# Latent attention: keys made for two heads and values for four heads at once, with the first values behind the first two score rows

## The chip, the cores and the metric

The kernel runs on one core of a Trainium2 chip. The metric is the device time of one execution in microseconds (us). The kernel is one program with its five engines (TensorE, VectorE, ScalarE, GpSimd, SyncE) programmed by hand: each engine has its own instruction list, which it works off in order, and they wait for one another through semaphores.

## The reference, cut to what matters

The model is two blocks; only the latent attention in the first layer of the first one is touched. For 1024 tokens and 8 heads:

```python
q = einsum('bsr,re->bse', rmsnorm(c_q, q_norm), w_uq)        # 256 -> 8 x (64 + 32)
kv = einsum('bsr,re->bse', rmsnorm(c_kv, kv_norm), w_ukv)    # 128 -> 8 x (64 + 64)
k_nope, v = kv[..., :64], kv[..., 64:]
s = (q_nope @ k_nope.T + rope(q_rope) @ rope(k_rope).T) * scale   # k_rope is one for all heads
p = softmax(where(causal, s, -inf))
y = p @ v
```

Everything before it (input projection, recurrent part) and after it (output product, layer norm, a state space layer, a second attention, a feed-forward part) stays as it is.

## The kernel before, in words

**Precision.** Every float32 operand of a product is split into a high part (rounded) and a low part (the rest), and three products are summed: high by high, low by high, high by low. ScalarE makes high parts by a copy, VectorE or GpSimd makes low parts by a subtraction. So a product of a head needs, after TensorE, a copy and a subtraction out of PSUM before it can be used.

**Weights.** They come in slabs of 128 x 1024 numbers, one DMA each from SyncE. GpSimd splits each (`split`, one cast and four subtractions) as soon as the slab two before it is released (semaphore `s_slab`). Each head has one slab: queries in tiles 0 and 1, and in tile 2 the 64 key columns and the 64 value columns of this head.

**The attention stage** is a loop over the heads u = 0 to 7, written out for each engine. "Body u" below is one pass of it. Body u computes the attention of head u and, between its parts, makes queries, keys and values of head u + 1 (`head_queries`, `head_keys`, `head_values`). Body 7 has no next head and makes none of these. Scores come in eight rows of 128 queries each (i = 0 to 7, `MLA_ROWS` gives their order, the long ones first). For a row: `score_rows` on TensorE, `neg_max` on VectorE, `exponentials` on ScalarE, `invert` on VectorE, `divide` on ScalarE. Then ten chunks (c = 0 to 9) of the probabilities are turned by TensorE (`turn_chunk`), split by ScalarE (`chunk_hi`) and VectorE (`chunk_lo`), and multiplied with the values (`chunk_values`). Chunks 0 to 3 need rows 0 and 1, chunks 4 to 6 rows 2 and 3, chunks 7 and 8 rows 4 and 5, chunk 9 rows 6 and 7.

**The order on TensorE** (in body u): score row 0, chunk 7 of the head before, row 1, chunk 8 of the head before, turn 9 of the head before, queries of u + 1, chunk 9 of the head before, row 2, turns 0 and 1, row 3, chunk 0, turn 2, keys of u + 1, chunk 1, turn 3, row 4, chunk 2, turn 4, row 5, chunk 3, turn 5, values of u + 1, chunk 4, turn 6, row 6, chunk 5, turn 7, row 7, chunk 6, turn 8. Body 0 has no parts of a head before. Queries, keys and values of head 0 stand ahead of the loop.

**The PSUM ring.** Score rows and the products for queries, keys and values share two pairs of banks, taken in turn (`MLA_RING`). A use waits until the use two before it is finished with (`ring_freed`): for a score row, until its exponential is done; for queries, until `q_turned` is done; for keys and values, until their low part is made (`s_kvl`).

**ScalarE in a body**: exponential 0, divide 0, chunk_hi 9 of before, exponential 1, divide 1, then chunk_hi 0, exponential 2, chunk_hi 1, exponential 3, chunk_hi 2, divide 2, `k_hi`, divide 3, chunk_hi 3, exponential 4, chunk_hi 4, exponential 5, chunk_hi 5, `q_hi`, `v_hi`, divides 4 and 5, chunk_hi 6 and so on. VectorE goes the same way, with `k_lo` behind `neg_max` 4 and `v_lo` behind `invert` 5. GpSimd makes the low part of the queries (`q_lo`).

**Keys.** A key tile (`KH`, `KL`) has the 64 own columns of the head in partitions 0 to 63 and the rotated common part in partitions 64 to 127. The common part is written once into each of two buffers ahead of the loop; head u uses buffer u % 2. `VM` holds the values of two heads, high and low part side by side.

## Time and profile before

| what | value |
|---|---|
| median of 3 runs | 2646.82 us (2643.38 to 2647.17) |
| span of the profiled execution | 2643.2 us |
| TensorE busy | 2572.9 us, 12880 matmuls |
| VectorE busy | 1599.2 us |
| ScalarE busy | 1001.6 us |
| GpSimd busy | 1140.9 us |
| attention stage, from the first queries to the last chunk | about 202 to 413 us of the span |

The profile gives no time of its own for the profiled execution beside its span; the three timed runs lie 0.2 to 4.0 us above the span. In the rows, "busy" of TensorE is the time in which at least one matmul was in flight, and matmuls overlap: a row's duration of one matmul is longer than the distance between two. A TensorE row of a timeline that says x2 or x8 is a run of that many matmuls, and its start against the start of the next row is the time they take.

### The profile page before, as it was taken

Reading aid. Unit: us, or ns where it says so; the run is one execution under the profiler, and the core shown is the slowest. Engines: PE = TensorE matmul, PEld = TensorE weight load, DVE = VectorE, ACT = ScalarE, POOL = GpSimd, SP = SyncE. Lnnn points to the kernel's source line nnn. Section 1 sums busy time; section 2 is a strip of 40 time slices with the busy share of each in tenths; the row PEclk is TensorE's granted clock in tenths of the full one; section 3 lists DMA queues with packets and bytes.
Section 4 is the critical chain, followed back from the end, with each engine's and each line's share of the span. In section 5 each row is a group of like instructions: output and inputs, shape, how many; then the busy total and the mean of one; then the engine's idle time right before and its main releaser. Section 6 shows DMA issues by size and latency. Waiting matters only on the chain.

```text
span 2643.2 us, 33209 instructions
## 1 busy us (share of the span) xinstructions
PE 2572.9 (97%) x12880; PEld 2055.9 (78%) x12880; DVE 1599.2 (61%) x1936; ACT 1001.6 (38%) x1434; POOL 1140.9 (43%) x1422
## 2 busy tenths in 40 slices
PE   8999999999999999999999999999999999999998
PEld 6877878687787787877776777767888888888886
DVE  6636663777647648557776455564455565555556
ACT  3527881436405315225365445563201111111132
POOL 4633344532432432432442222214565557655653
PEclk9999999999999999999999999999999999999999
DMA  3110002212112112111230010003111111111312
GB/s 139 48 51 27 24 25 90 86 59 100 52 55 73 58 49 71 66 59 66 90 112 24 25 33 25 33 17 104 56 49 48 48 56 56 54 43 49 120 47 80
DMA packets 44822, 156.36 MB, mean 59 GB/s; under 512 B 4928, under 2 KB 5312, under 8 KB 44672
## 3 DMA queue, kind: packets, MB, share of 16 engines
q1 hardware_dynamic: 31392, 110.11, 12.8%
q10 hardware_dynamic: 13280, 44.17, 4.6%
q8 instruction: 103, 1.69, 0.3%
q14 instruction: 47, 0.39, 0.0%
HBM read 141.55 MB, written 12.71 MB: 58 GB/s over the span
## 4 chain that ended last, share of the span: by engine, by line
PE 85%; DVE 8%; ACT 4%; issue 2%; POOL 1%; ACTq 0%; DVEq 0%; POOLq 0%
PE PS L784 38%; PE PS L1459 13%; PE PS L1485 10%; PE PS L1114 4%; PE PS L1021 3%; PE PS L1507 2%; PE PS L1347 1%; PE PS L920 1%; PE PS L1330 1%; PE PS L1147 1%; PE PS L1157 1%; PE PS L1151 1%; PE PS L934 1%; PE PS L1370 1%; DVE mla_neg_max L2397 1%
## 5 line engine op out<-in xcount | busy, mean ns | idle before, releaser
L637 POOL CAST w_hi<-w_stage 128x1024 fp32r<-128x1024 f32 x130 | 145.0, 1115 | 1048.4 <-PE PS L784 758.2
L640 POOL TENSOR_TENSOR w_lo<-w_stage,w_hi 128x256 fp32r<-128x256 f32 x520 | 492.9, 979 | 10.4
L784 PE MATMUL PS<-XH,w_hi 128*128 128x512 f32 x1216 | 386.7, 399 | 9.0 <-ACT ssd_z L1899 3.3
L784 PE MATMUL PS<-XL,w_hi 128*128 128x512 f32 x1216 | 375.9, 390 | 0.0
L784 PE MATMUL PS<-XH,w_lo 128*128 128x512 f32 x1216 | 375.4, 390 | 0.0
L784 PEld LDWEIGHTS PS<-XH,w_hi 128*128 128x128 f32 x1216 | 221.5, 188 | 65.4 <-issue 12.9
L784 PEld LDWEIGHTS PS<-XH,w_lo 128*128 128x128 f32 x1216 | 228.3, 188 | 48.7
L784 PEld LDWEIGHTS PS<-XL,w_hi 128*128 128x128 f32 x1216 | 228.3, 188 | 48.6
L711 POOL TENSOR_TENSOR w_lo<-w_stage,w_hi 128x256 fp32r<-128x256 f32 x260 | 220.1, 853 | 0.0
L707 POOL CAST w_hi<-w_stage 128x256 fp32r<-128x256 f32 x260 | 125.7, 486 | 185.6 <-PE PS L1459 108.2
L1459 PE MATMUL PS<-raw_hi,w_hi 128*128 128x512 f32 x512 | 158.2, 390 | 0.0
L1459 PE MATMUL PS<-raw_hi,w_lo 128*128 128x512 f32 x512 | 157.8, 389 | 0.0
L1459 PE MATMUL PS<-raw_lo,w_hi 128*128 128x512 f32 x512 | 157.7, 389 | 0.0
L1485 PE MATMUL PS<-ffn_u_hi,w_hi 128*128 128x512 f32 x392 | 152.6, 389 | 0.0
L1485 PE MATMUL PS<-ffn_u_hi,w_lo 128*128 128x512 f32 x392 | 152.6, 389 | 0.0
L1485 PE MATMUL PS<-ffn_u_lo,w_hi 128*128 128x512 f32 x392 | 152.6, 389 | 0.0
L3032 DVE TENSOR_TENSOR H<-H,PS 128x512 f32<-128x512 f32 x140 | 96.1, 686 | 76.9 <-PE PS L1485 76.9
L2973 DVE SCALAR_TENSOR_TENSOR ffn_t<-PS,root 128x1024 f32<-128x1024 f32 x32 | 39.2, 1225 | 154.2 <-PE PS L1459 145.0
L2176 ACT ACTIVATE ffn_t<-ffn_t 128x1024 f32<-128x1024 f32 x32 | 34.0, 1061 | 240.1 <-DVE ffn_t L2973 240.1
L1459 PEld LDWEIGHTS PS<-raw_hi,w_hi 128*128 128x128 f32 x512 | 96.1, 188 | 20.3 <-issue 0.5
L1459 PEld LDWEIGHTS PS<-raw_lo,w_hi 128*128 128x128 f32 x512 | 96.1, 188 | 19.9
L1459 PEld LDWEIGHTS PS<-raw_hi,w_lo 128*128 128x128 f32 x512 | 96.1, 188 | 19.9
(459 smaller groups left out, 5421.5 us busy)
## 6 DMA issues: line engine op xcount, KB each, us to landing
w_stage<-w SPq DMA_DIRECT2D x202, 512.0 KB, 3.4
ssd_sum_rows<-sums_kept ACTq DMA_DIRECT2D x32, 512.0 KB, 3.7
H<-x_t ACTq DMA_DIRECT2D x8, 512.0 KB, 8.3
pj_kept<-ple_proj_tiles ACTq DMA_DIRECT2D x8, 512.0 KB, 2.6
h_kept<-H ACTq DMA_DIRECT2D x8, 512.0 KB, 3.0
H<-h_kept ACTq DMA_DIRECT2D x4, 1024.0 KB, 5.5
out_t<-out_tiles SPq DMA_DIRECT2D x16, 256.0 KB, 2.1
x_again<-x_t ACTq DMA_DIRECT2D x12, 256.0 KB, 3.1
```

Source lines behind the costliest of these rows:

```text
L637: nc.gpsimd.tensor_copy(w_hi[:, slot, :, :], w_stage[:, slot, :, :]).then_inc(s_w_hi, 1)
L640: nc.gpsimd.tensor_tensor(w_lo[:, slot, k:k + 2, :], w_stage[:, slot, k:k + 2, :], w_hi[:, slot, k:k + 2, :].bitcast(F32), ALU.subtract).t ...
L707: nc.gpsimd.tensor_copy(ring(w_hi, e), src).then_inc(s_eh.sem, 1)
L711: nc.gpsimd.tensor_tensor(ring(w_lo, e), src, ring(w_hi, e).bitcast(F32), ALU.subtract).then_inc(done, count)
L784: mm = nc.tensor.matmul(outs[:, half, :], wt[:, slot, k, :], a[:, k - first, half * HB:(half + 1) * HB], start=(k == whole[0] and wt is w_ ...
L1021: mm = nc.tensor.matmul(PS[:, 2 * (n % 2) + half, :], wt[:, n % 2, k, :], a[:, k, half_cols(half)], start=(k == 0 and wt is w_hi and a is ...
L1114: mm = nc.tensor.matmul(PS[:, half, :], wt[:, n % 2, k, :], a[:, k, half * HB:(half + 1) * HB], start=(k == 0 and wt is w_hi and a is XH), ...
L1459: mm = nc.tensor.matmul(PS[:, 2 * (c % 2) + half, :], ring(wt, e + k // 2, k % 2), a[:, k, half * HB:(half + 1) * HB], start=(k == 0 and w ...
L1485: mm = nc.tensor.matmul(PS[:, BANK[j], :], ring(wt, e + i, k), a[:, ACTS_AT[j], k, :], start=(j not in BEFORE and k == 0 and wt is w_hi an ...
L1507: mm = nc.tensor.matmul(PS[:, 4 + 2 * e + half, :], ring(wt, e0 + k // 2, k % 2), a[:, t, half * HB:(half + 1) * HB], start=(first and wt ...
L2973: v.scalar_tensor_tensor(out=FT[:, c % 2, :], in0=flat(c % 2), scalar=0.0, in1=RSQ[:, :], op0=ALU.max, op1=ALU.mult).then_inc(s_ue, 1)
L3032: v.tensor_tensor(dst, dst, src, ALU.add).then_inc(s_dr, 1)
```

## The change

The weights of a head's slab are laid out anew on the host: tile 2 holds the keys of two heads (slabs of heads 0, 2, 4, 6), tiles 3 and 4 hold the values of four heads (slabs of heads 0 and 4). The number of slabs and their size stay.

- `head_keys` runs for even heads only and fills all 128 rows of the output: head u in partitions 0 to 63, head u + 1 in 64 to 127. Its six matmuls keep their 512 columns. `k_hi` and `k_lo` then make two copies and two subtractions, one for each head. There are three key buffers (head u uses u % 3), so a third copy and a third subtraction of the common rotated part come ahead of the loop.
- `head_values` runs for heads 0 and 4. It has two parts (j = 0, 1) of 512 tokens each, with 12 matmuls of 256 columns per part in place of 24 of 64 columns per head. Each part takes a turn in the ring and is split by itself. The values of head 4 go to a tile of their own (`VM4`), since head 3 is not finished with when they are made; those of 5 to 7 take the places of 0 to 2.
- The values of head 0 to 3 are made in body 0 behind score row 1 and ahead of the queries of head 1, no longer ahead of the loop; `v_hi(0)` stands behind `divide(0, 1)` on ScalarE, `v_lo(0)` behind `invert(0, 1)` and ahead of `q_turned(1)` on VectorE.
- The last product that reads a head's slab releases it: keys or values for even heads, the queries for odd heads.
- The rotated key part waits at another address (`KF`) until it is copied.

```diff
-MLA_RING = [("q", 0), ("k", 0), ("v", 0)]
+KEY_HEADS, VALUE_HEADS = 2, 4
+MLA_RING = [("q", 0), ("k", 0)]
+MLA_PARTS = [("rope", 0, 0), ("rope", 1, 0), ("rope", 2, 0), ("k", 0, 0), ("k", 0, 1)]
 for _u in range(MLA_H):
     for _i in range(8):
         MLA_RING.append((_i, _u))
-        if _i in (1, 3, 5) and _u + 1 < MLA_H:
-            MLA_RING.append(({1: "q", 3: "k", 5: "v"}[_i], _u + 1))
+        if _i == 1 and _u == 0:
+            MLA_RING += [("v", 0, 0), ("v", 0, 1)]
+            MLA_PARTS += [("v", 0, 0), ("v", 0, 1)]
+        if _u + 1 == MLA_H:
+            continue
+        if _i == 1:
+            MLA_RING.append(("q", _u + 1))
+        if _i == 3 and (_u + 1) % KEY_HEADS == 0:
+            MLA_RING.append(("k", _u + 1))
+            MLA_PARTS += [("k", _u + 1, _e) for _e in range(KEY_HEADS)]
+        if _i == 5 and (_u + 1) % VALUE_HEADS == 0:
+            MLA_RING += [("v", _u + 1, 0), ("v", _u + 1, 1)]
+            MLA_PARTS += [("v", _u + 1, 0), ("v", _u + 1, 1)]
...
+        def value_places(u):
+
+            if u == 0:
+                return [(VM, 0, 0, VALUE_HEADS)]
+            return [(VM4, 0, 0, 1), (VM, 0, 1, VALUE_HEADS)]
...
             def head_values(u):
-                n, b = N_HEADS + u, 2 * mla_pair(("v", u))
-                ring_freed(("v", u))
-                for a, wt in ((CKH, w_hi), (CKH, w_lo), (CKL, w_hi)):
-                    for t in range(KT):
-                        mm = nc.tensor.matmul(PS[:, b, 64 * t:64 * t + 64], a[:, t * P:(t + 1) * P], wt[:, n % 2, 2, 64:128],
-                                              start=(t == 0 and a is CKH and wt is w_hi), stop=True, skip_group_check=True)
-                mm.then_inc(s_slab, 1)
+                if u % VALUE_HEADS:
+                    return
+                n = N_HEADS + u
+                for j in range(2):
+                    b = 2 * mla_pair(("v", u, j))
+                    ring_freed(("v", u, j))
+                    for a, wt in ((CKH, w_hi), (CKH, w_lo), (CKL, w_hi)):
+                        for t in range(4):
+                            tok = slice((4 * j + t) * P, (4 * j + t + 1) * P)
+                            mm = nc.tensor.matmul(PS[:, b + t // 2, t % 2 * 256:t % 2 * 256 + 256], a[:, tok],
+                                                  wt[:, n % 2, 3:5, :].rearrange("p a b -> p (a b)"),
+                                                  start=(t % 2 == 0 and a is CKH and wt is w_hi), stop=True, skip_group_check=True)
+                    mm.then_inc(s_hp if j == 0 else s_slab, 1)
...
             head_queries(0)
             head_keys(0)
-            head_values(0)
             for u in range(MLA_H):
                 more = u + 1 < MLA_H
                 score_rows(u, 0)
                 if u:
                     chunk_values(u - 1, 7)
                 score_rows(u, 1)
+                if u == 0:
+                    head_values(0)
...
             def k_hi(u):
-                act.wait_ge(s_hp, 2 * u + 2)
-                nc.scalar.activation(KH[0:64, u % 2, :], flat(mla_pair(("k", u)))[0:64, :], ACT.Copy).then_inc(s_kvh, 1)
+                if u % KEY_HEADS:
+                    return
+                head_product(act, "k", u)
+                for e in range(KEY_HEADS):
+                    nc.scalar.activation(KH[0:64, (u + e) % 3, :], flat(mla_pair(("k", u)))[64 * e:64 * e + 64, :], ACT.Copy).then_inc(s_kvh, 1)
...
             def v_hi(u):
-                act.wait_ge(s_slab, N_HEADS + u + 1)
-                nc.scalar.activation(VM[:, u % 2, :, 0:64], PS[:, 2 * mla_pair(("v", u)), :].rearrange("p (t d) -> p t d", d=64),
-                                     ACT.Copy).then_inc(s_kvh, 1)
+                if u % VALUE_HEADS:
+                    return
+                for j in range(2):
+                    if j == 0:
+                        head_product(act, "v", u, 0)
+                    else:
+                        act.wait_ge(s_slab, N_HEADS + u + 1)
+                    if u == 0 and j == 0:
+                        act.wait_ge(s_kvl, 3)
+                    for t, at_, h0, h1 in value_places(u):
+                        done = nc.scalar.activation(value_part(t, at_, h1 - h0, j, 0), value_bank(u, j, h0, h1), ACT.Copy)
+                    done.then_inc(s_kvh, 1)
...
-            v_hi(0)
             nc.scalar.preload_act_table_set("natural_log_exp_and_others")
...
                 if u:
                     low_part(u - 1, 0)
                 else:
+                    v_hi(0)
                     gated_hi(2)
...
                 invert(u, 1)
+                if u == 0:
+                    v_lo(0)
                 if more:
                     q_turned(u + 1)
```

## Rows read from the trace of the kernel before

**Rows 1.** The page: busy time of each engine, share of the span, instructions.

```profile
PE 2572.9 (97%) x12880; PEld 2055.9 (78%) x12880; DVE 1599.2 (61%) x1936; ACT 1001.6 (38%) x1434; POOL 1140.9 (43%) x1422
```

**Rows 2.** Windows: stretch, length, busy time (instructions) by engine, granted clock, DMA.

```profile
210.00:235.00 25.00, 24.26 (x148) 19.89 (x148) 14.60 (x26) 21.39 (x36) 7.76 (x8) 0.93 0.09 30
260.00:285.00 25.00, 24.16 (x167) 20.50 (x166) 17.20 (x33) 20.14 (x39) 11.11 (x9) 1.00 0.07 22
```

**Rows 3.** Timeline, TensorE, body 2: chunk 9, row 3, turns 4, 5, 7.

```profile
267.81 0.34 PE L949 MATMUL PS<-mla_p_hi,mla_v_hi_lo 128*128 128x256 f32 x2
...
270.12 0.60 PE L920 MATMUL PS<-mla_k_hi,mla_q_hi 128*128 128x512 f32 x2
...
276.50 0.66 PE L934 MATMUL PS<-CN,mla_p 128*128 128x128 f32 x4 [0.60 <-ACT mla_p L1684]
...
278.47 0.62 PE L934 MATMUL PS<-CN,mla_p 128*128 128x128 f32 x4
...
283.49 0.66 PE L934 MATMUL PS<-CN,mla_p 128*128 128x128 f32 x4
```

**Rows 4.** Timeline, TensorE, body 7: the same five places.

```profile
391.20 0.45 PE L949 MATMUL PS<-mla_p_hi,mla_v_hi_lo 128*128 128x256 f32 x2 [2.35 <-DVE mla_p_lo L2408]
...
395.21 0.60 PE L920 MATMUL PS<-mla_k_hi,mla_q_hi 128*128 128x512 f32 x2
...
400.91 0.66 PE L934 MATMUL PS<-CN,mla_p 128*128 128x128 f32 x4 [0.30 <-ACT mla_p L1684]
...
402.64 0.61 PE L934 MATMUL PS<-CN,mla_p 128*128 128x128 f32 x4
...
405.98 0.66 PE L934 MATMUL PS<-CN,mla_p 128*128 128x128 f32 x4
```

**Rows 5.** Timeline, TensorE, body 2: keys, chunk 1, turn 3; values, chunk 4.

```profile
272.34 0.70 PE L898 MATMUL PS<-ckv_hi,w_hi 128*64 128x512 f32 x2
...
273.80 0.40 PE L949 MATMUL PS<-mla_p_hi,mla_v_hi_lo 128*128 128x256 f32 x2
...
274.28 0.49 PE L934 MATMUL PS<-CN,mla_p 128*128 128x128 f32 x3
...
278.85 1.06 PE L907 MATMUL PS<-w_hi,ckv_hi 128*128 128x64 f32 x8
...
281.53 0.48 PE L949 MATMUL PS<-mla_p_hi,mla_v_hi_lo 128*128 128x256 f32 x2
```

**Rows 6.** Timelines of ScalarE and VectorE, body 2, and ScalarE, body 7.

```profile
274.61 1.01 ACT L1668 ACTIVATE mla_k_hi<-PS 64x1024 fp32r<-64x1024 f32 x1
275.52 0.93 ACT L1684 ACTIVATE mla_p<-mla_p,mla_sums 128x768 f32<-128x768 f32 x1
...
280.09 1.06 ACT L1664 ACTIVATE mla_q_hi<-mla_q 128x1024 fp32r<-128x1024 f32 x1
281.73 0.60 ACT L1672 ACTIVATE mla_v_hi_lo<-PS 128x512 fp32r<-128x512 f32 x1 [0.58 <-PE PS L907]
282.22 1.22 ACT L1684 ACTIVATE mla_p<-mla_p,mla_sums 128x384 f32<-128x384 f32 x2
...
275.88 1.21 DVE L2388 TENSOR_TENSOR mla_k_lo<-PS,mla_k_hi 64x1024 fp32r<-64x1024 f32 x1
...
404.26 0.62 ACT L1684 ACTIVATE mla_p<-mla_p,mla_sums 128x384 f32<-128x384 f32 x1
```

**Rows 7.** Ahead of the loop: rope subtractions, `q_turned(0)`, score row 0 of head 0.

```profile
L2379 DVE TENSOR_TENSOR mla_k_lo<-key_rope,mla_k_hi x2: 1223/1641/2059, 201.8 to 202.9; 64x1024 fp32r<-64x1024 f32 x2
...
205.22 1.23 DVE L2383 SCALAR_TENSOR_TENSOR mla_q<-PS,trig 128x1024 f32<-128x1024 f32 x1 [0.27 <-PE PS L784]
...
210.02 0.68 PE L920 MATMUL PS<-mla_k_hi,mla_q_hi 128*128 128x512 f32 x2 [0.65 <-POOL mla_q_lo L654]
```

**Rows 8.** Body 0: score row 2, the divide of row 1, `q_turned(1)`.

```profile
217.48 0.56 PE L920 MATMUL PS<-mla_k_hi,mla_q_hi 128*128 128x512 f32 x2
...
217.66 1.15 ACT L1684 ACTIVATE mla_p<-mla_p,mla_sums 128x1024 f32<-128x1024 f32 x1 [0.23 <-DVE mla_sums L2403]
...
217.62 1.23 DVE L2383 SCALAR_TENSOR_TENSOR mla_q<-PS,trig 128x1024 f32<-128x1024 f32 x1
```

More of the change, by code:

```diff
@@ L170 @@
         MLA_RING.append((_i, _u))
-        if _i in (1, 3, 5) and _u + 1 < MLA_H:
-            MLA_RING.append(({1: "q", 3: "k", 5: "v"}[_i], _u + 1))
+        if _i == 1 and _u == 0:
[11 more added lines that the diff above has]
+            MLA_PARTS += [("v", _u + 1, 0), ("v", _u + 1, 1)]
+HEAD_PRODUCTS = [_k for _u in range(MLA_H) for _k in
+                 (("q", _u), ("k", _u), ("v", _u, 0)) if _u % {"q": KEY_HEADS, "k": VALUE_HEADS, "v": VALUE_HEADS}[_k[0]] == 0]
 MLA_TURN = {_key: _n for _n, _key in enumerate(MLA_RING)}
@@ L177, in mla_high, with mla_part, key_part @@
     return MLA_HIGHS.index(key) + 1
+def mla_part(kind, u, e=0):
+    return MLA_PARTS.index((kind, u, e)) + 1
+def key_part(u):
+    return mla_part("k", u - u % KEY_HEADS, u % KEY_HEADS)
 def mla_pair(key):
@@ L751, in _, with head_product, value_weights, value_part @@
                 plain_slab(n)
+        def head_product(eng, *key):
+            if key in HEAD_PRODUCTS:
+                eng.wait_ge(s_hp, HEAD_PRODUCTS.index(key) + 1)
+            else:
+                eng.wait_ge(s_slab, N_HEADS + key[1] + 1)
+        def value_places(u):
+            if u == 0:
+                return [(VM, 0, 0, VALUE_HEADS)]
+            return [(VM4, 0, 0, 1), (VM, 0, 1, VALUE_HEADS)]
+        def value_weights(u, kt):
+            if u < VALUE_HEADS:
+                return VM[:, u, kt, :]
+            return VM4[:, 0, kt, :] if u == VALUE_HEADS else VM[:, u - VALUE_HEADS - 1, kt, :]
+        def value_part(t, first, heads, j, o):
+            return t[:, first:first + heads, 4 * j:4 * j + 4, o:o + 64].rearrange("p h t d -> p t h d")
+        def value_bank(u, j, h0, h1):
+            return flat(mla_pair(("v", u, j))).rearrange("p (t h d) -> p t h d", t=4, d=64)[:, :, h0:h1, :]
         class Tiles:
@@ L874, in ring_freed @@
                     return
-                kind, u = MLA_RING[turn - 2]
+                kind, u = MLA_RING[turn - 2][:2]
                 if kind == "q":
@@ L888, in head_queries @@
                 ring_freed(("q", u))
-                product(pair(mla_pair(("q", u))), n, CQH, CQL, range(2), ready=None if u else (s_llo, 0)).then_inc(s_hp, 1)
+                mm = product(pair(mla_pair(("q", u))), n, CQH, CQL, range(2), ready=None if u else (s_llo, 0))
+                mm.then_inc(s_hp if ("q", u) in HEAD_PRODUCTS else s_slab, 1)
             def head_keys(u):
+                if u % KEY_HEADS:
+                    return
                 n, b = N_HEADS + u, 2 * mla_pair(("k", u))
@@ L948, in chunk_values @@
                         late = P if e and p == i else 0
-                        mm = nc.tensor.matmul(PS[:, b, q0 + late:q0 + 2 * P], VM[:, u % 2, 2 * p + e, :],
+                        mm = nc.tensor.matmul(PS[:, b, q0 + late:q0 + 2 * P], value_weights(u, 2 * p + e),
                                               src[:, n % 4, 2 * P * e:2 * P * (e + 1) - late],
@@ L1652, in _ @@
             act.wait_ge(s_kr, 3)
-            for b in range(2):
+            for b in range(3):
                 nc.scalar.activation(KH[64:128, b, :], KF[64:128, :], ACT.Copy).then_inc(s_kvh, 1)
@@ L2376, in _ @@
                 v.tensor_tensor(lo, CQ[:, j, :], hi.bitcast(F32), ALU.subtract).then_inc(s_llo, 1)
-            for b in range(2):
+            for b in range(3):
                 dve.wait_ge(s_kvh, b + 1)
@@ L2386, in k_lo @@
             def k_lo(u):
[L2387 to L2393 removed]
+                if u % KEY_HEADS:
+                    return
+                for e in range(KEY_HEADS):
+                    at_ = (u + e) % 3
+                    dve.wait_ge(s_kvh, mla_part("k", u, e))
+                    v.tensor_tensor(KL[0:64, at_, :], flat(mla_pair(("k", u)))[64 * e:64 * e + 64, :], KH_f[0:64, at_, :], ALU.subtract).then_inc(s_kvl, 1)
+            def v_lo(u):
+                if u % VALUE_HEADS:
+                    return
+                for j in range(2):
+                    dve.wait_ge(s_kvh, mla_part("v", u, j))
+                    for t, at_, h0, h1 in value_places(u):
+                        done = v.tensor_tensor(value_part(t, at_, h1 - h0, j, 64), value_bank(u, j, h0, h1),
+                                               value_part(t, at_, h1 - h0, j, 0).bitcast(F32), ALU.subtract)
+                    done.then_inc(s_kvl, 1)
             def neg_max(u, i):
@@ L2416, in _ @@
             k_lo(0)
-            v_lo(0)
             v.memset(SM[:, 5, 0:1], 0.0).then_inc(s_evac[1], MLA_H // 2)
```

40 lines of the change are left out of this document (21 added, 19 removed).

## The prediction

> **What bounds the kernel now.** The page comes first. TensorE is busy for 97% of the span [rows 1], so the obvious reading is that TensorE time taken out is time won. The change touches one stage only, the latent attention (about 202 to 412 us of 2643), so I then read that stage by windows [rows 2]. In a steady stretch ScalarE is busy 20 of 25 us and VectorE 17 of 25. Neither is full, but both work in a fixed order, and TensorE's order alternates between matmuls that need nothing and matmuls that wait for them. The third view is TensorE's timeline of one steady pass, the body of head 2 [rows 3]. Its one wait in these rows looks small: 0.60 us before `turn_chunk(2, 4)`, for a divide on ScalarE.
>
> The row that decides is elsewhere. The body of head 7 makes no queries, keys or values for a next head, since there is none, so it is a body with this filling work taken out. I compare the same places in both bodies, from the score row of i = 3 on [rows 3, 4]:
> - score row 3 to chunk turn 4: 276.50 - 270.12 = 6.38 us with a key product between, 400.91 - 395.21 = 5.70 us without. Saved: 0.68 us, though the key product takes 1.46 us of TensorE.
> - chunk turn 4 to chunk turn 5: 1.97 against 1.73 us. Saved: 0.24 us. Score row 5 waits for a key split in one and not in the other.
> - chunk turn 5 to chunk turn 7: 5.02 us with the value product (2.68 us), 3.34 us without.
> So the filling products sit largely in time that the softmax chain (scores, maximum, exponential, divide, turn, high part, low part) takes anyway. TensorE looks 97% busy because the filling fits, not because it is the bound.
>
> **The change, TensorE's work.** A head's 24 value matmuls take 281.53 - 278.85 = 2.68 us, 112 ns each for 64 columns; four 256-column matmuls with the same kind of weights take 274.28 - 273.80 = 0.48 us, 120 ns each [rows 5]. Eight value products (21.4 us) become 48 matmuls of 256 columns (5.8 us). Four key products of eight go, at 273.80 - 272.34 = 1.46 us each: 5.8 us. In all 21.4 us less TensorE work. On this the Trainium skill would differ: TensorE: Matmul & The Clock Gate, "Back-to-back issue gap", prices a matmul by its columns, N / 2.4 + 2.5 ns, which is 29 ns for 64 columns and 109 ns for 256; by that (an estimate) the values would cost 5.6 us before and 5.2 after and save nothing. The measured 112 ns of these very instructions contradicts it, and nothing below uses it.
>
> **What of it reaches the end, body by body** ("body u" computes head u and makes the products of head u + 1).
>
> Bodies 2, 4 and 6 lose keys and values but keep the queries. They become like body 7 plus one `q_hi` on ScalarE. There `divide(7, 4)` starts at 404.26 [rows 6]; `q_hi` (1.0 us) would stand in its place, and the two divides (1.22 us together [rows 6]) would end at 406.45, so turn 7 is 406.45 - 402.64 = 3.81 us after turn 5 and not 5.02. Gain per body 0.68 + 0.24 + 1.21 = 2.13 us; three bodies 6.4 us.
>
> Bodies 1 and 5 keep a key product, now with two halves to split, and lose the values. ScalarE issues a second `k_hi` (0.91 us from one start to the next [rows 6]) ahead of `divide(u, 3)`, for which turn 4 already waits: +0.9 us. VectorE's second `k_lo` (1.21 us [rows 6]) stands in front of `chunk_lo(3)`, and score row 5 waits for both splits: another 0.15. Everything to exponential 5 and `q_hi` is then 1.05 us late. Behind `q_hi`, the wait for the values (0.58 us idle) and `v_hi` (0.49 us until the divide) are gone: 1.07 back. Net 0.0 to 0.2, I take 0.1 each.
>
> Body 3 has both: two key splits (+1.05 to `q_hi`), and two value parts of 1024 columns. The values of head 4 go to another tile than those of 5 to 7, so each part is two copies and two subtractions. ScalarE then has about 1.15 us per part before the divides, where it had 0.58 + 0.49 in all. `q_hi` ended at 281.15 in body 2, so ends at 282.2 here; 2.3 for the parts and 1.2 for the divides make 285.7, so turn 7 comes at 285.75 and not 283.49. VectorE needs 1.3 us per part, and score rows 6 and 7 now wait for these subtractions in the ring of PSUM pairs (284.75 and 286.05). Loss 2.4 us.
>
> Body 0 is the place that matters. Today the first values run while the chain query product, `q_turned`, `q_hi`, `q_lo` is under way (TensorE waits 0.65 us at the end [rows 7]), so they cost nothing there. After the change:
> - A third rope part costs ScalarE one copy near 187 us, where it waits anyway, but VectorE one subtraction more before `q_turned(0)`. Such a one takes 1.22 to 2.06 us [rows 7]; VectorE has 0.27 us of idle there. I take the short one, since the long one ran beside GpSimd's work: 0.95 us later. `q_hi`, `q_lo` and score row 0 move by it, from 210.02 to 210.95. TensorE idles from 206.5 on.
> - Part of the 25 us from 210 was at half clock (1.2 GHz): 0.93 granted on average [rows 2], and the first score rows are slow in it. Row 0 then lies in it wholly (0.15 us longer), so the softmax of the first two rows is 1.1 us late: `divide(0, 1)` ends at 218.8 [rows 8] + 1.1 = 219.9.
> - Now the new chain. `v_hi(0)` stands behind `divide(0, 1)` on ScalarE: 1.0 us for 1024 columns, 220.9. `v_lo` 1.23 us (as `q_turned`, also 1024 columns out of PSUM [rows 8]), 222.1. The ring of two PSUM pairs makes `head_queries(1)` wait for the split of the first value half, which held its pair. The queries are twelve matmuls of the kind of which six make a key product (1.46 us): 2.9, so 225.0. Score row 2 waits for the second half (223.3, earlier) and so starts at 225.0, where it started at 217.48 [rows 8]. Before, queries 1 waited only for the exponential of row 0. That is 7.5 us; 0.2 of it comes back because chunk turn 0, right behind row 2, had to wait for that divide's end at 218.81 and now need not. 7.3 us late at score row 3.
> - From there it is a body without keys and values: 2.13 back. Net loss 5.2 us.
> Behind score row 2 in TensorE's queue stand chunk turn 0 and everything of head 0, so nothing fills this.
>
> GpSimd gets its slabs' release earlier for odd heads and 10 us later for head 0. The next slab (about 4 us to split) is wanted a body later: nothing. No DMA is added or removed, and the weights loaded are as many.
>
> **Sum.** +5.2 (body 0) + 2.4 (body 3) - 0.2 (1, 5) - 6.4 (2, 4, 6) = +1.0 us. Against the profiled span of 2643.2 this is 2644.2; the median of the runs shown is 2646.82, 3.6 us over that span, so 2647.8. Behind the attention TensorE has products back to back, so a shift is handed to the end unchanged.
> Bounds: the long rope subtraction +0.85. The value copy at twice its 512-column row (0.60 us [rows 6], so 1.20 for 1024) +0.2. Body 3 with no cover +1. On the good side: the second key split and body 3's value split wholly under other waits, -1.0 each for bodies 1 and 5 and -2.4 for body 3. That is 2643.4 to 2649.9 without the clock.
>
> **Rivals.**
> (a) TensorE is the bound after all. For it: 97% busy, and waits that look small. Then bodies 1, 5 give 2.68 each, bodies 2, 4, 6 give 4.14 each, body 3 nothing, and body 0 loses 7.3 - 4.14 = 3.2: 17.8 - 3.2 = 14.6 us faster, 2632. Against it: from score row 3 to turn 7, body 7 takes 10.77 us and body 2 takes 13.37, only 2.60 less for 4.14 us of matmuls missing, and one copy fewer on ScalarE in it. Chance 0.12.
> (b) Slower: the clock. Body 7 had TensorE idle for 2.35 us, and then a stretch at half clock in which score row 2 and turns 0, 1 took 395.21 - 391.20 = 4.01 us, where body 2 took 270.12 - 267.81 = 2.31: 1.7 us per such stretch [rows 3, 4]. After the change body 0 has two new idle times (before the second value half, and 2 us before queries 1), and bodies 2, 4, 6 have 2 us more idle each. One stretch, in queries 1, is as likely as not and costs 1.2 to 1.7 us: 2649. It takes three to be over the 5.3 us that count as slower; four give 2647.8 + 6.8 = 2654.6. Against that: in bodies 2, 4, 6 the idle comes in pieces of 0.5 to 1 us. Chance of three or more 0.12. The Trainium skill (the same page, "Why this matters for your kernels") also warns of idle gaps between bursts of matmuls as the cause of drops in mid-kernel; this trace shows it at 391 us.
> (c) The first values hurt less than I say, because ScalarE reaches them earlier or the ring wait is shorter, and bodies 1, 3, 5 come out at their good bounds (-4.4): 4 to 9 us better, 2639 to 2644. Chance 0.14.
> My forecast, 2644 to 2652 with at most two new stretches at half clock: 0.62.
>
> **Numbers.** 2647.8 is the likeliest case. The range 2640 to 2654 holds the forecast, most of (c) and part of (b), and leaves (a) out. Over 0.2% (5.3 us, about what measurement tells from no change) faster, below 2641.5, are (a) and a third of (c): 0.17. Slower, above 2652.1, is (b) and the forecast's edge: 0.16. Within: 0.67.
>
> **What the new profile must show.** Queries 1 start near 222 us with a wait for the first value subtraction; score row 2 near 225. From score row 3 to chunk turn 7, bodies 2, 4 and 6 take about 11.2 us (now 13.4), 1 and 5 about as now, body 3 about 15.6. Value matmuls 48, near 120 ns apart. If bodies 2, 4, 6 take about 9.2 there, (a) is right; if half-clock stretches appear in them, (b). I am wrong in the main if ScalarE and VectorE wait for TensorE in body 2 between turn 5 and turn 7.

## The result, and the profile after

Over 19 runs of each, the changed kernel takes 2651.33 us (median; 2646.75 to 2653.68) and the kernel before 2646.80 (2643.06 to 2649.16). The ratio is 1.0020, 95% interval 1.0014 to 1.0026: slower by 3.7 to 6.9 us; the two medians themselves lie 4.5 us (0.17%) apart. The forecast was 2647.8 in a range of 2640 to 2654, with "within 0.2%" as the likeliest. The time lies in the range, 3.5 us above the forecast, and the ratio at the edge of 0.2%, on the slower side. For the change itself the forecast was +1.0 us. Below, one of the eleven runs of x1_rope (9895 us) and one of x3_fill (2879 us) were slow and are in no ratio.

The page of the changed kernel, its first lines (they answer to [rows 1]):

```profile
span 2651.4 us, 32872 instructions
...
PE 2564.2 (97%) x12712; PEld 2044.7 (77%) x12712; DVE 1602.6 (60%) x1935; ACT 1003.8 (38%) x1433; POOL 1142.0 (43%) x1422
```

There are 168 matmuls fewer, all of them in the attention, and the span is longer. TensorE is still "97% busy". Nothing on this page says what happened, so the stage has to be read.

Windows of the changed kernel (stretch, length, busy time and count of TensorE, its weight loads, VectorE, ScalarE, GpSimd, granted clock, DMA). The first two answer to [rows 2]; the last three each hold a stretch at half clock (0.50), in bodies 0, 1 and 3, with some time at full clock around it:

```profile
210.00:235.00 25.00, 20.09 (x95) 16.22 (x95) 13.12 (x18) 16.21 (x23) 5.54 (x6) 0.80 0.14 43
...
260.00:285.00 25.00, 23.01 (x139) 19.27 (x139) 17.27 (x32) 20.57 (x42) 9.08 (x8) 0.93 0.07 22
...
224.00:229.00 5.00, 5.00 (x19) 3.97 (x18) 1.67 (x2) 0.00 (x0) 1.53 (x3) 0.66 0.32 105
...
262.00:266.00 4.00, 4.00 (x23) 3.65 (x21) 2.12 (x5) 2.69 (x6) 0.22 (x1) 0.57 0.02 6
...
309.00:315.00 6.00, 5.80 (x33) 5.42 (x33) 2.89 (x7) 3.99 (x9) 1.33 (x1) 0.72 0.00 0
```

In the first window TensorE is busy for 20.1 us and not 24.3, with 95 matmuls and not 148: this is the hole at the start of the stage. ScalarE and VectorE do less in it too. The granted clock is 0.80 and not 0.93.

TensorE's timeline of the changed kernel: body 0 first (keys 0, score row 0, the two halves of the first values, queries 1, score row 2), then body 2 (score row 3, chunk turns 4, 5, 7, as in [rows 3]), then body 3 (chunk turn 4, the values of heads 4 to 7, the chunk behind them, turn 7):

```profile
206.21 0.61 PE L949 MATMUL PS<-ckv_hi,w_lo 128*128 128x512 f32 x2
211.74 1.11 PE L977 MATMUL PS<-mla_k_hi,mla_q_hi 128*128 128x512 f32 x2 [4.92 <-POOL mla_q_lo L678]
...
217.04 1.17 PE L963 MATMUL PS<-w_hi,ckv_hi 128*128 128x256 f32 x4
...
219.84 0.74 PE L963 MATMUL PS<-w_hi,ckv_hi 128*128 128x256 f32 x4 [0.68 <-ACT mla_p L1748]
...
223.48 0.70 PE L832 MATMUL PS<-cq_hi,w_hi 128*128 128x512 f32 x2 [1.94 <-POOL w_lo L664]
...
224.99 1.06 PE L832 MATMUL PS<-cq_hi,w_hi 128*128 128x512 f32 x2
...
227.55 0.74 PE L977 MATMUL PS<-mla_k_hi,mla_q_hi 128*128 128x512 f32 x2
...
278.27 0.61 PE L977 MATMUL PS<-mla_k_hi,mla_q_hi 128*128 128x512 f32 x2
...
283.98 0.66 PE L991 MATMUL PS<-CN,mla_p 128*128 128x128 f32 x4 [0.30 <-ACT mla_p L1754]
...
285.71 0.61 PE L991 MATMUL PS<-CN,mla_p 128*128 128x128 f32 x4
...
289.55 0.66 PE L991 MATMUL PS<-CN,mla_p 128*128 128x128 f32 x4 [0.59 <-ACT mla_p L1754]
...
308.41 0.66 PE L991 MATMUL PS<-CN,mla_p 128*128 128x128 f32 x4 [1.65 <-ACT mla_p L1754]
...
311.66 1.20 PE L963 MATMUL PS<-w_hi,ckv_hi 128*128 128x256 f32 x4
...
315.00 0.64 PE L963 MATMUL PS<-w_hi,ckv_lo 128*128 128x256 f32 x4
315.48 0.40 PE L1006 MATMUL PS<-mla_p_hi,mla_v_hi_lo 128*128 128x256 f32 x2
...
317.93 0.66 PE L991 MATMUL PS<-CN,mla_p 128*128 128x128 f32 x4
```

Body 0 holds two waits that were not there: 4.92 us before score row 0 (0.65 before, [rows 7]) and 1.94 us before queries 1. In body 2 everything is where it was forecast: row 3 to turn 7 takes 289.55 - 278.27 = 11.28 us.

The other engines' timelines of the changed kernel:

```profile
202.04 4.89 DVE L2449 TENSOR_TENSOR mla_k_lo<-key_rope,mla_k_hi 64x1024 fp32r<-64x1024 f32 x3
206.95 1.23 DVE L2453 SCALAR_TENSOR_TENSOR mla_q<-PS,trig 128x1024 f32<-128x1024 f32 x1
...
222.11 2.35 DVE L2470 TENSOR_TENSOR mla_v_hi_lo<-PS,mla_v_hi_lo 128x1024 fp32r<-128x1024 f32 x2 [2.13 <-ACT mla_v_hi_lo L1742]
...
221.07 1.92 ACT L1742 ACTIVATE mla_v_hi_lo<-PS 128x1024 fp32r<-128x1024 f32 x2
...
204.24 4.63 POOL L664 TENSOR_TENSOR w_lo<-w_stage,w_hi 128x256 fp32r<-128x256 f32 x4
209.34 2.35 POOL L678 TENSOR_TENSOR mla_q_lo<-mla_q,mla_q_hi 128x1024 fp32r<-128x1024 f32 x1 [0.47 <-ACT mla_q_hi L1722]
```

The wait of queries 1 is put down to `w_lo` by the profile, but GpSimd began the next `w_lo` only at 222.72, for the slab of head 2, and those that queries 1 need ended at 208.9. The first of the two `v_lo` (start 222.11, half of 2.35 us) ends at 223.3, and queries 1 start at 223.48: that is the ring of PSUM pairs, as forecast.

Where the difference lies is seen best from the length of each body. A body is taken here from the start of score row 0 of one head to that of the next; the last column is the start of score row 7 of head 7, all in us, each kernel from its own profiled execution.

| kernel | row 0, head 0 | row 2, head 0 | body 0 | 1 | 2 | 3 | 4 | 5 | 6 | row 7, head 7 |
|---|---|---|---|---|---|---|---|---|---|---|
| before | 210.02 | 217.48 | 24.91 | 25.49 | 24.82 | 24.84 | 24.80 | 24.80 | 24.83 | 406.39 |
| after | 211.74 | 227.55 | 31.03 | 25.85 | 22.68 | 28.38 | 22.72 | 25.11 | 22.71 | 412.41 |
| x1_rope | 211.21 | 225.70 | 29.38 | 25.77 | 22.72 | 28.37 | 22.71 | 25.07 | 22.73 | 410.16 |
| x2_ahead | 211.47 | 218.34 | 22.37 | 25.57 | 22.71 | 26.95 | 22.78 | 25.90 | 22.72 | 402.36 |
| x3_fill | 211.31 | 224.66 | 28.23 | 25.57 | 22.68 | 26.98 | 22.79 | 25.70 | 22.70 | 407.84 |
| x4_keys_only | 212.68 | 220.67 | 24.44 | 26.73 | 23.90 | 27.54 | 23.88 | 26.08 | 23.90 | 411.31 |
| x5_values_only | 211.23 | 225.48 | 30.05 | 24.32 | 23.61 | 25.73 | 23.70 | 23.66 | 23.61 | 407.70 |
| x6_before_third | 210.10 | 218.13 | 24.80 | 24.78 | 24.11 | 24.13 | 24.09 | 24.12 | 24.12 | 402.13 |
| x7_late | 209.90 | 216.74 | 22.54 | 25.83 | 22.73 | 28.36 | 22.68 | 25.16 | 22.74 | 402.14 |
| x8_late_qhi | 210.06 | 216.91 | 22.04 | 25.46 | 22.23 | 26.83 | 22.23 | 25.23 | 22.21 | 398.39 |
| x9_before_qhi | 209.82 | 217.54 | 25.20 | 25.49 | 24.77 | 24.80 | 24.77 | 24.80 | 25.99 | 407.95 |
| x10_values_best | 210.27 | 217.12 | 22.62 | 23.83 | 23.13 | 25.58 | 23.12 | 23.14 | 23.13 | 397.03 |

From before to after: row 0 of head 0 +1.72, body 0 +6.12, body 3 +3.54, bodies 1 and 5 +0.67 together, bodies 2, 4, 6 -6.34 together, body 7 +0.3. That is +6.0 us at row 7 of head 7. The two spans differ by 8.2; another 1.6 us came between 546 and 583 us, where the changed kernel's execution had a stretch at half clock (549 to 553 us) among dense products; the kernel before had one at 528 to 532 us, where it cost nothing that shows. The rest came in crumbs. The medians differ by 4.5 us only, so what lies outside the stage belongs to these two executions, and the stage is what is to be explained. Stretches at half clock also come and go between executions of one kernel: the changed kernel's 19 go from 2646.75 us at a granted clock of 0.997 to 2653.68 at 0.992, and the profiled one (2653.21, 0.992) is the second slowest of them.

### The profile page after: what moved, and what is told of

Its sections match the earlier page's. It is cut to its first block, busy times and chain, and to the rows that moved or that the text cites. A ratio compares the mean times of both kernels' runs of the same rounds, so it can differ in the third digit from the quotient of the medians.

```text
span 2651.4 us, 32872 instructions
## 1 busy us (share of the span) xinstructions
PE 2564.2 (97%) x12712; PEld 2044.7 (77%) x12712; DVE 1602.6 (60%) x1935; ACT 1003.8 (38%) x1433; POOL 1142.0 (43%) x1422
## 3 DMA queue, kind: packets, MB, share of 16 engines
q8 instruction: 101, 1.65, 0.3%
## 4 chain that ended last, share of the span: by engine, by line
PE 84%; DVE 9%; ACT 5%; issue 2%; POOL 1%; ACTq 0%; DVEq 0%; POOLq 0%
PE PS L832 38%; PE PS L1517 13%; PE PS L1543 10%; PE PS L1172 4%; PE PS L1079 2%; PE PS L1565 2%; PE PS L1405 1%; PE PS L977 1%; PE PS L1388 1%; PE PS L1205 1%; PE PS L1215 1%; PE PS L1209 1%; PE PS L1428 1%; PE PS L991 1%; DVE mla_neg_max L2476 1%
```

## The experiments

All medians are of runs on one chip beside runs of the kernel before; that kernel's median in the same comparison stands behind "against". It differs from one comparison to the next (2645.46 to 2646.80), so two kernels of different comparisons are set side by side by their distances from it: the changed kernel lies 4.5 us above it. Each ratio is to the kernel before, with its 95% interval.

### Body 0: the rope part, the order, the clock

**x1_rope** moves the third rope subtraction behind `q_turned(0)` on VectorE.

```diff
+            rope_low(0)
+            rope_low(1)
...
             q_turned(0)
+            rope_low(2)
             k_lo(0)
```

> The changed kernel with the third rope subtraction moved on VectorE from ahead of q_turned(0) to behind it, where VectorE waited 2.0 us for the first k_hi. Theory (the subtraction delays the whole head 0 chain): q_turned(0) starts near 205.5 and not 206.95 us, score row 0 near 210.2 and not 211.74, and score row 2 of head 0 1.5 us earlier than 227.55; total 1 to 2 us below the changed kernel, so about 3 us over the kernel before. Rival (score row 0 is not what orders body 0, the clock is): row 0 earlier, row 2 and the total unchanged.

Measured: 2651.42 us against 2645.48, ratio 1.0021 (1.0012 to 1.0031). `q_turned(0)` came back to 205.46, as expected, yet score row 0 started at 211.21, only 0.5 us earlier than in the changed kernel. GpSimd's timeline of this kernel says why:

```profile
204.20 4.65 POOL L664 TENSOR_TENSOR w_lo<-w_stage,w_hi 128x256 fp32r<-128x256 f32 x4
208.81 2.34 POOL L678 TENSOR_TENSOR mla_q_lo<-mla_q,mla_q_hi 128x1024 fp32r<-128x1024 f32 x1
```

`q_lo` stands behind four `w_lo` on GpSimd. These took 3.68 us in the kernel before (from 203.95) and take 4.65 here, as in the changed kernel (4.63), since a third VectorE subtraction from SBUF runs beside them in both. Moving it by one instruction only changes which of two nearly equally late engines is waited for. Score row 2 still came 1.85 us earlier (225.70), and most of that is the clock: in this execution queries 1 hold no stretch at half clock and take 225.70 - 222.88 = 2.82 us, where the changed kernel's took 4.07. The median shows no gain, though the stage was 2.2 us shorter in the profiled execution; by time alone this run is inconclusive.

**x2_ahead** makes the first values ahead of the loop, in the two PSUM pairs that the chunk turns use later, outside the ring; `v_hi(0)` stands before the first exponential, and the `v_lo` behind the first two maxima. Three copies on ScalarE that are not part of the attention (`gated_hi`, 1.05 us each) also move to later places in body 0.

```diff
+    if key[:2] == ("v", 0):
+        return 2 + key[2]
     return (MLA_TURN[key] + 1) % 2
...
             head_keys(0)
+            head_values(0)
...
             k_hi(0)
+            v_hi(0)
...
                 neg_max(u, 0)
+                if u == 0:
+                    v_lo(0, [0])
```

> The changed kernel with the first values (heads 0 to 3) made ahead of the loop again, in the two PSUM pairs that are free until the first chunk turns, so outside the ring; their copies stand on ScalarE ahead of exponential 0, their subtractions on VectorE behind neg_max 0 and 1. Theory (placing them behind score row 1, where queries 1 wait for the split, costs 7 to 8 us): queries 1 wait for exponential 0 alone, score row 2 starts near 219 to 220 us and not 227.55; total 7 to 8 us below the changed kernel, so 2 to 4 us below the kernel before. Rival (the loss sits in the later bodies or the clock): score row 2 earlier by less than 3 us, total as the changed kernel.

Measured: 2641.92 us against 2645.48, ratio 0.9988 (0.9979 to 0.9997): 3.6 us below the kernel before, and so 8.1 below the changed kernel, by the distances. TensorE's and ScalarE's timelines of this kernel:

```profile
211.47 0.68 PE L980 MATMUL PS<-mla_k_hi,mla_q_hi 128*128 128x512 f32 x2 [2.05 <-POOL mla_q_lo L679]
...
215.46 0.70 PE L833 MATMUL PS<-cq_hi,w_hi 128*128 128x512 f32 x2 [0.91 <-ACT mla_p L1752]
...
218.34 0.56 PE L980 MATMUL PS<-mla_k_hi,mla_q_hi 128*128 128x512 f32 x2
...
210.97 1.94 ACT L1746 ACTIVATE mla_v_hi_lo<-PS 128x1024 fp32r<-128x1024 f32 x2
```

Queries 1 wait for an exponential again and start 8.0 us earlier than in the changed kernel; score row 2 comes 9.2 us earlier. The two copies of 1.94 us are the same work at 210.97 as at 221.07, but here ScalarE had nothing else to do. The price of body 0 is thus the place of the first values, and not their form. Part of it is the clock: in the stage this execution has no stretch at half clock before body 5, and the next run shows what that alone is worth.

**x3_fill** keeps the order of the changed kernel and puts 42 matmuls whose results nobody reads into TensorE's idle time of body 0.

```diff
             head_keys(0)
+            fill(22)
...
                 if u == 0:
+                    fill(4)
                     head_values(0)
+                    fill(9)
```

(The other 7 stand between the two halves of the values.)

> The changed kernel with 42 extra matmuls of 512 columns in TensorE's idle times of body 0 (22 behind the keys of heads 0 and 1, 4 and 7 around the value halves, 9 ahead of queries 1), results unused. Theory (the waits for the split cost most, half clock the rest): no half-clock stretch before 228 us, score rows 0 and 1 take 1.2 to 1.4 us each and not 2.5 to 2.8, score row 2 of head 0 starts near 225 and not 227.55; total 2 to 3 us below the changed kernel. Rival (the clock is the whole loss): score row 2 near 220, total 7 us below.

Measured: 2647.76 us against 2645.48, ratio 1.0006 (0.9997 to 1.0016): 2.3 us above the kernel before, where the changed kernel is 4.5 above. TensorE's timeline of this kernel:

```profile
206.16 5.15 PE L1022 MATMUL PS<-ckv_hi,cq_hi 128*128 128x512 f32 x22
...
221.85 0.67 PE L832 MATMUL PS<-cq_hi,w_hi 128*128 128x512 f32 x2
...
224.66 0.45 PE L979 MATMUL PS<-mla_k_hi,mla_q_hi 128*128 128x512 f32 x2
```

More work on TensorE made the kernel faster. Queries 1 take 224.66 - 221.85 = 2.81 us and not 227.55 - 223.48 = 4.07, and they start 1.6 us earlier, since rows 0 and 1 and the values ran at full clock too. Score row 2 is 2.9 us earlier, 0.4 of which is already there at row 0. So of body 0's lateness at score row 2 (10.1 us) about 2.5 to 3 belong to the clock and the rest to the waits; x2_ahead, at full clock there like this one, has its score row 2 another 6.3 us earlier. Body 3 has no half-clock stretch here, nor in x2_ahead, and takes 26.98 us and not 28.38.

### Does TensorE work in the bodies cost anything?

**x6_before_third** is the kernel before with one of each three value matmuls; it leaves out both products with a low part.

```diff
-                for a, wt in ((CKH, w_hi), (CKH, w_lo), (CKL, w_hi)):
+                for a, wt in ((CKH, w_hi),):
```

> The kernel before, with one in three of the value matmuls left (high by high alone; the low products are left out, so the values are rounded). TensorE has 1.8 us less in each of bodies 0 to 6, 12.5 us in all; ScalarE and VectorE do the same work. Theory (the softmax chain on ScalarE and VectorE is the bound, and of the value product only ScalarE's wait of 0.58 us shows): 0.5 to 0.7 us less per body, 3.5 to 5 us in all. Rival (TensorE is the bound): 1.8 us per body, 12 us in all.

Measured: 2641.09 us against 2645.48, ratio 0.9983 (0.9974 to 0.9992): 4.4 us. Bodies 1 to 6 became 0.7 us shorter each for the 1.8 us of TensorE work missing in each (two thirds of 2.68). About 40% of what is taken off TensorE comes back: rival (a), for which all of it should have, is refuted by this run, and by bodies 2, 4, 6 of the changed kernel.

### Keys alone, values alone

**x4_keys_only** makes the keys for two heads and the values per head as before.

```diff
-MLA_RING = [("q", 0), ("k", 0)]
+MLA_RING = [("q", 0), ("k", 0), ("v", 0)]
...
-                 (("q", _u), ("k", _u), ("v", _u, 0)) if _u % {"q": KEY_HEADS, "k": VALUE_HEADS, "v": VALUE_HEADS}[_k[0]] == 0]
+                 (("q", _u), ("k", _u)) if _u % {"q": 1, "k": KEY_HEADS}[_k[0]] == 0]
```

> One part alone: keys for two heads at once as in the change (three key buffers, third rope part ahead of the loop), values made per head as before, those of head 0 ahead of the loop. Theory: bodies 0, 2, 4, 6 save 0.9 us each (no key product, no key split before the divide), bodies 1, 3, 5 lose 1.05 each (two splits), the rope part costs 1.5: +1.0 us against the kernel before, within 0 to 2.5. Rival (TensorE is the bound): four key products of 1.46 us less, 4 to 6 us below the kernel before.

Measured: 2653.05 us against 2646.42, ratio 1.0028 (1.0019 to 1.0037): 6.6 us slower, well above what I expected. Bodies 2, 4, 6 gained the 0.9 us expected. The miss has two parts. One is at the start, in TensorE's timeline of this kernel:

```profile
208.08 1.08 PE L953 MATMUL PS<-w_hi,ckv_hi 128*128 128x64 f32 x8 [1.41 <-DVE mla_q L2432]
...
212.68 1.09 PE L966 MATMUL PS<-mla_k_hi,mla_q_hi 128*128 128x512 f32 x2 [0.93 <-DVE mla_k_lo L2441]
```

With the values of head 0 in the ring again, score row 0 takes the pair that the keys held, and so waits for the second key split too; it starts 2.66 us later than before. The other part is bodies 1, 3 and 5: 1.24, 2.70 and 1.28 us longer, where the second key split had been priced at 1.05. Body 3 holds a stretch at half clock; bodies 1 and 5 hold none, so 1.2 to 1.3 us is what the second split costs.

**x5_values_only** makes the keys per head and the values for four.

```diff
-KEY_HEADS, VALUE_HEADS = 2, 4
+KEY_HEADS, VALUE_HEADS = 1, 4
```

(with the second part of the keys' list left out and one head's keys in each slab.)

> The other part alone: values for four heads as in the change (first ones behind score row 1), keys made per head as before. Theory: against the changed kernel bodies 0, 2, 4, 6 are 0.9 us longer and bodies 1, 3, 5 are 1.0 to 1.4 us shorter, so no change of the total by more than 1 us: 2650 to 2652. Rival (TensorE is the bound): 5.8 us over the changed kernel, 2656.

Measured: 2648.16 us against 2646.42, ratio 1.0011 (1.0002 to 1.0020), about 3 us below the changed kernel by the distances, where I had expected at most 1. Bodies 1 to 6 take 144.6 us in all, and 147.4 with paired keys. So pairing the keys gives nothing in this kernel: a body without them gains 0.9 us, and its neighbour pays 1.2 for the second split even at full clock (25.57 against 24.32 in body 1 and 26.95 against 25.73 in body 3, x2_ahead against this kernel). The clock adds to it. With paired keys TensorE waits 1.65 us before chunk turn 4 in bodies 1, 3 and 5, and each such kernel has a stretch at half clock in one of them or more; with keys per head (this kernel, x10_values_best) no wait in bodies 1 to 6 is longer than 0.9 us, and there is no such stretch.

### What a better order gives

**x7_late** is x2_ahead with the third rope subtraction inside body 0, behind `invert(0, 2)`; the rotated part waits for it at another address.

```diff
-MLA_PARTS = [("rope", 0, 0), ("rope", 1, 0), ("rope", 2, 0), ("k", 0, 0), ("k", 0, 1)]
+MLA_PARTS = [("rope", 0, 0), ("rope", 1, 0), ("k", 0, 0), ("k", 0, 1)]
...
+                else:
+                    rope_low(2)
+                    dve.wait_ge(s_kvl, mla_part("rope", 2))
                 chunk_lo(u, 2)
```

> The kernel x2_ahead with the third rope subtraction moved on VectorE into body 0 (behind invert(0, 2)), away from GpSimd's split of the weights and from the head 0 chain; the rotated part waits at another free address. Theory: VectorE's third subtraction both delayed q_turned(0) and slowed GpSimd's four w_lo from 3.7 to 4.7 us, behind which q_lo(0) stands; now w_lo take 3.7 us again, score row 0 starts at 210.0 to 210.2 as in the kernel before (x2_ahead: 211.5), total 1.3 us below x2_ahead, 2640.5. Rival (only the place ahead of q_turned counts, which x1_rope already showed to be worth 0.5 us at score row 0): score row 0 at 211, total 0.5 us below x2_ahead.

Measured: 2641.91 us against 2646.42, ratio 0.9983 (0.9974 to 0.9992). GpSimd's and TensorE's timelines of this kernel:

```profile
203.78 3.70 POOL L669 TENSOR_TENSOR w_lo<-w_stage,w_hi 128x256 fp32r<-128x256 f32 x4
...
209.90 0.67 PE L984 MATMUL PS<-mla_k_hi,mla_q_hi 128*128 128x512 f32 x2 [0.66 <-POOL mla_q_lo L683]
```

The `w_lo` are back at 3.70 us and score row 0 at 209.90, as in the kernel before. That settles the start: with the third subtraction out of the way both engines are as quick as they were. Little of the 1.5 us is left at the end of the profiled execution (score row 7 of head 7 at 402.14 and 402.36), though: bodies 1 and 3 took 25.83 and 28.36 us, each with a stretch at half clock, where x2_ahead had 25.57 and 26.95 without one; body 5, with one in both, took 25.16 and 25.90. By the medians x7_late is 4.5 us below the kernel before and x2_ahead 3.6, and their intervals overlap: against x2_ahead the total stays unresolved.

**x8_late_qhi** is x7_late with `q_hi` ahead of exponential 5 on ScalarE.

```diff
                 chunk_hi(u, 4)
+                if more:
+                    q_hi(u + 1)
                 exponentials(u, 5)
...
-                    q_hi(u + 1)
```

> The kernel x7_late with q_hi on ScalarE moved ahead of exponential 5, where ScalarE waits 1.1 us for neg_max 5. Theory (ScalarE's order between exponential 5 and the divides of rows 4 and 5 sets when chunk turn 7 comes): bodies 0, 2, 4, 6 become 0.4 to 0.5 us shorter, bodies 1 and 5 0.5 to 1.0: 2.5 to 3.5 us below x7_late, 2637.5. Rival (TensorE is the bound once the first values are moved): no change.

Measured: 2638.01 us against 2646.42, ratio 0.9968 (0.9956 to 0.9981). ScalarE's timeline of body 2 of this kernel:

```profile
274.21 1.07 ACT L1730 ACTIVATE mla_q_hi<-mla_q 128x1024 fp32r<-128x1024 f32 x1
275.16 0.70 ACT L1754 ACTIVATE mla_p<-PS,mla_neg_max 128x512 f32<-128x512 f32 x1
...
276.30 0.64 ACT L1760 ACTIVATE mla_p<-mla_p,mla_sums 128x384 f32<-128x384 f32 x1
277.27 0.72 ACT L1760 ACTIVATE mla_p<-mla_p,mla_sums 128x512 f32<-128x512 f32 x1 [0.33 <-DVE mla_sums L2492]
```

`q_hi` fills the time in which ScalarE waited for the maximum of row 5, and is gone from in front of the two divides. Bodies 2, 4, 6 take 22.2 us and not 22.7. Bodies 1 and 5, where I had expected 0.5 to 1.0 less, changed by 0.37 less and 0.07 more. Body 3 took 1.5 less; it has no stretch at half clock here, and x7_late had one.

**x9_before_qhi** makes the same move in the kernel before, and nothing else.

> The kernel before with q_hi on ScalarE moved ahead of exponential 5 and nothing else. Theory: there ScalarE must wait for the value product behind q_hi anyway (0.58 us idle before v_hi), so the time q_hi leaves is filled by that wait and the divides come when they came: bodies 24.8 us as before, total within 1 us of the kernel before. Rival (q_hi's place is worth its time in any kernel): 0.5 us per body, 3 us in all, as from x7_late to x8_late_qhi.

Measured: 2646.29 us against 2645.46, ratio 1.0002 (0.9993 to 1.0011); bodies 1 to 5 unchanged within 0.05 us. (Body 6 took 1.16 us more; it holds a stretch at half clock that the kernel before does not have.) There the value product stands between, and ScalarE waits for it whatever comes first [rows 6]. The move pays only once that product is gone from the body, so the gain in x8_late_qhi rests on the wide values.

**x10_values_best** takes what gained and leaves out what did not: keys per head, with two key buffers and two rope parts; values for four heads, the first ones ahead of the loop as in x2_ahead; `q_hi` ahead of exponential 5.

```diff
-KEY_HEADS, VALUE_HEADS = 2, 4
+KEY_HEADS, VALUE_HEADS = 1, 4
...
-            for b in range(3):
+            for b in range(2):
```

> Keys one head at a time as in the kernel before (two key buffers, two rope parts), values for four heads, the first ones ahead of the loop in the free PSUM pairs, q_hi ahead of exponential 5. Theory (pairing the keys is worth nothing, since what a body without a key product saves, a body with two key splits loses, and the rope part costs on top): score row 0 at 210.0, bodies 1, 2, 4, 5, 6 at 23.2 us (body 1 23.8), body 3 at 25.3, total 1 to 3 us below x8_late_qhi, about 2636, 10 us below the kernel before. Rival (the four key products saved count for something): above x8_late_qhi by 2 us or more.

Measured: 2635.64 us against 2645.46, ratio 0.9963 (0.9950 to 0.9977): 9.8 us faster than the kernel before and the lowest median of all, though its interval overlaps that of x8_late_qhi. TensorE's timeline of its start:

```profile
210.27 0.68 PE L980 MATMUL PS<-mla_k_hi,mla_q_hi 128*128 128x512 f32 x2 [0.65 <-POOL mla_q_lo L679]
...
214.24 0.69 PE L833 MATMUL PS<-cq_hi,w_hi 128*128 128x512 f32 x2 [0.88 <-ACT mla_p L1752]
...
217.12 0.56 PE L980 MATMUL PS<-mla_k_hi,mla_q_hi 128*128 128x512 f32 x2
```

The first values are covered by the wait for `q_lo`, as they were before the change, and queries 1 follow the first exponential. Its bodies 2, 4, 6 are 0.9 us longer than those of x8_late_qhi, its bodies 1, 3, 5 are 1.6, 1.3 and 2.1 us shorter: the keys once more.

## Why the prediction was right or wrong

**TensorE is not the bound: right.** Comparing bodies 2 and 7 foretold what a body gains when its filling goes. Of x6_before_third's missing work 40% came back, and x3_fill became faster by added work.

**TensorE's work: right.** 48 value matmuls of 256 columns, four in 315.48 - 315.00 = 0.48 us, 120 ns each. TensorE's busy time fell by 8.7 us and not by 21.4; stretches at half clock lengthen the other matmuls, and how much of the gap that explains was not measured apart. Against the 112 ns for 64 columns the prediction sets a formula of the Trainium skill (TensorE: Matmul & The Clock Gate, "Back-to-back issue gap"). That section gives it for a single matmul by itself and says that it counts too little for few columns, where weight loads come between. Here every matmul has its weight load (12880 of each), so the 112 ns contradict that formula taken by itself, but not the section.

**Bodies 2, 4, 6: right.** Forecast 2.13 us less each, measured 2.14, 2.08 and 2.12. Row 3 to turn 7 took 11.28 us (forecast 11.24), turn 5 to turn 7 took 3.84 (forecast 3.81).

**Bodies 1 and 5: forecast too low by 0.4 each.** Forecast 0.1 less, measured 0.36 and 0.31 more. Both hold a stretch at half clock (from 262 us in the windows above). In x2_ahead, where body 1 has none, it took 0.08 more than before. So in body 1 the sum of ScalarE's parts was off by 0.2 and the clock made the rest. For body 5 this is not shown: every kernel with paired keys and wide values has a stretch in it.

**Body 3: mechanism right, 1.1 us too low.** Forecast +2.4, measured +3.54. The half-clock stretch lies on the value matmuls themselves (309 to 315 us, mean granted clock 0.72). In x2_ahead and x3_fill, without it, body 3 took 2.1 us more than before, and score row 3 to turn 7 took 15.64 us (forecast 15.6). The forecast's own places, 285.75 against 283.49, give 2.3 and not 2.4.

**Body 0: the mechanism right, two terms mis-sized.** This is the step that failed in size. The chain of the forecast is there link by link: `v_hi(0)` behind `divide(0, 1)`, `v_lo`, the ring, queries 1, score row 2. Forecast 222.1 and 225.0, measured 223.48 and 227.55; score row 3 was 10.0 us late and not 7.3. Of the 2.7 us, 2.55 are there at score row 2, and they are these:
- "I take the short one ... 0.95 us later". The third rope subtraction took 4.89 us less the 3.2 of two: 1.7 us. After VectorE's 0.27 us of idle that is 1.4 and not 0.95, so my upper bound was nearer; a start 0.3 us later comes on top. And the subtraction cost GpSimd 0.95 us as well, which I hadn't looked for: x1_rope removed the one and met the other; x7_late removed both and won the 1.5 us at row 0. Against the forecast score row 0 was 0.8 us late (211.74 and not 210.95).
- The clock. I let row 0 lie at half clock and left the rest of the stretch and queries 1 at full. With 4.92 us of idle ahead, rows 0 and 1 and the first value matmuls all ran at half clock, and `divide(0, 1)` ended another 0.5 us late. It came again in queries 1, which took 4.07 us and not 2.9: 1.2 us. With 0.1 us in the hand-overs between, these make up the 2.55 us at score row 2.

The 2.1 us given back behind score row 3 were right (10.02 late there, 7.84 at body 1).

**Rival (b), the clock: true by its count, wrong by its price.** I had named queries 1 as the likely place, and there it was. There were stretches in bodies 1, 3 and 5 as well, though not in 2, 4, 6 where I had looked for them, and the one on the first score rows was twice as long as before. So the profiled execution had at least four new stretches, and my forecast had allowed for two at most. But I had priced each like body 7's, at 1.7 us. The one in queries 1 cost 1.2, that in body 1 0.3, that in body 3 1.4. The price goes by the place: in body 5 of x2_ahead and x3_fill the stretch begins 0.9 to 1.1 us behind the start of chunk turn 4, in the changed kernel 1.9, and score row 3 to turn 7 takes 14.48, 14.28 and 13.67 us. Without a stretch it took 13.46 in body 1 of x2_ahead. That the time still fell within the forecast's 2644 to 2652 was in part luck: two misses, in the number of stretches and in the price of each, worked against each other.

**Rival (a): refuted. Rival (c): nothing of it came;** the first values hurt more than I said, and no body came out at its good bound.

**The slabs and the DMAs: nothing, as forecast;** no wait for either ends last in the stage. `w_lo`, named before queries 1, is not it.

Left open: why the stretches at half clock moved between kernels that differ only in body 0 (x2_ahead has none in body 1, x7_late has one), and so whether x7_late's earlier start is worth anything by itself. Each kernel was profiled in one execution, and the granted clock differs between executions of one kernel, so the move may belong to the execution and not to the kernel. What the rope part cost in the median was not resolved by x1_rope either.

## What to carry to other kernels

Look for a pass of the loop that lacks the filling work, as head 7 does here: the difference between it and a steady pass is what that filling is worth, and it was right to 0.05 us where "97% busy" was wrong by a factor of two. Before work is batched, ask for its first batch and not for its average one: where it stands in the fixed order of the engines that split it, which buffer ring it passes, and whether it still lies under a wait that nothing else fills. Then undo each half alone, since here the wide values, with the order around them redone, were worth 10 us, and the paired keys nothing.
